# A two-block network on one core: loads, matmul order and PSUM banks of the first five projection slabs changed

## The reference, cut to what matters

```python
def rms_norm(x, g):
    xf = x.astype(jnp.float32)
    y = xf * lax.rsqrt(jnp.mean(xf * xf, axis=-1, keepdims=True) + NORM_EPS)
    return (y * g.astype(jnp.float32)).astype(x.dtype)

def hybrid_layer(x, ...):
    hn = rms_norm(x, ln1)
    proj = hn @ w_in          # 1024 -> 2824 columns: queries, keys, values, mLSTM inputs and gates
    mq, mk, mv, sq, sk, sv, xqk, xv, xo, xi, xf = jnp.split(proj, idx, axis=-1)
    ...
    x = x + jnp.concatenate([y_moba, y_mlstm, y_swa], axis=-1) @ w_out
    u = rms_norm(x, ln2) @ w_up
    return x + jnp.square(jax.nn.relu(u)) @ w_down
```

## Time and profile before

| | us |
|---|---|
| median of three runs (1414.11 to 1416.08) | 1415.93 |
| the profiled execution | 1415.56 |
| its span, from the first instruction to the last | 1413.8 |
| TensorE busy | 1389.7 (98%) |
| VectorE busy | 1119.7 (79%) |
| ScalarE busy | 845.9 (60%) |
| GpSimd busy | 101.3 (7%) |

### The profile page before, as it was taken

One profiled execution on the slowest core, in us unless ns is written; L12 is line 12 of the kernel. 1 busy time (PEld: TensorE's weight loads), 2 busy tenths in 40 slices (PEclk: granted clock), 3 DMA queues, 4 the chain that ended last, 5 costly groups with the idle time before them and its releaser, 6 DMA issues.

```text
span 1413.8 us, 25601 instructions
## 1 busy us (share of the span) xinstructions
PE 1389.7 (98%) x10325; PEld 1301.2 (92%) x10325; DVE 1119.7 (79%) x1693; ACT 845.9 (60%) x1309; POOL 101.3 (7%) x157
## 2 busy tenths in 40 slices
PE   8999999999999999999999999999999999999997
PEld 7898888889888888889999999998999999999986
DVE  7898888889898888887777788777778777876653
ACT  6776776345876875356576475454465664754442
POOL 2000111100000011103100000000031000000000
PEclk9999999999999999999999999999999999999999
DMA  9643999986545999969955678887699456777662
GB/s 261 163 142 105 279 271 279 293 230 166 147 133 165 294 265 290 299 195 260 305 149 150 184 220 238 241 250 214 187 262 301 140 161 181 222 218 231 183 187 65
DMA packets 472692, 301.32 MB, mean 213 GB/s; under 512 B 15084, under 2 KB 453872, under 8 KB 472448
## 3 DMA queue, kind: packets, MB, share of 16 engines
q1 hardware_dynamic: 455056, 239.57, 60.7%
q0 software_dynamic: 16704, 58.29, 12.6%
q10 hardware_dynamic: 816, 1.84, 0.4%
HBM read 289.43 MB, written 1.05 MB: 205 GB/s over the span
## 4 chain that ended last, share of the span: by engine, by line
PE 85%; DVE 9%; ACT 4%; issue 2%; DMA 1%; SPq 0%; ACTq 0%; DVEq 0%
PE acc L2093 15%; PE acc L2094 15%; PE acc L2095 15%; PE mx L2110 10%; PE acc L2110 8%; PE mx L2111 5%; PE acc L2111 4%; DVE w_lo L1176 3%; DVE ada_acc L1266 1%; ACT w_hi L587 1%; PE acc L2125 1%; PE acc L2126 1%; PE acc L2127 1%; PE mx L2539 1%; PE acc L2231 1%
## 5 line engine op out<-in xcount | busy, mean ns | idle before, releaser
L1176 DVE TENSOR_TENSOR w_lo<-raw,w_hi 128x1024 fp32r<-128x1024 f32 x450 | 542.6, 1220 | 125.2 <-ACT w_hi L587 122.8
L587 ACT ACTIVATE w_hi<-raw 128x1024 fp32r<-128x1024 f32 x450 | 465.1, 1052 | 135.9 <-DMA raw<-in_w_in 63.4
L2093 PE MATMUL acc<-h,w_hi 128*128 128x256 f32 (+1 forms) x1696 | 484.5, 286 | 7.7 <-DVE w_lo L1176 5.5
L2094 PE MATMUL acc<-h,w_hi 128*128 128x256 f32 (+1 forms) x1696 | 475.6, 280 | 0.0
L2095 PE MATMUL acc<-h,w_lo 128*128 128x256 f32 (+1 forms) x1696 | 474.0, 280 | 0.0
L2093 PEld LDWEIGHTS acc<-h,w_hi 128*128 128x128 f32 x1696 | 319.4, 188 | 14.6 <-issue 7.8
L2094 PEld LDWEIGHTS acc<-h,w_hi 128*128 128x128 f32 x1696 | 319.7, 189 | 2.6 <-issue 2.4
L2095 PEld LDWEIGHTS acc<-h,w_lo 128*128 128x128 f32 x1696 | 320.2, 189 | 0.0
L2110 PE MATMUL mx<-u,w_hi 128*128 128x512 f32 x864 | 302.2, 392 | 0.0
L2111 PE MATMUL mx<-u,w_lo 128*128 128x256 f32 x864 | 243.5, 282 | 0.0
L2110 PEld LDWEIGHTS mx<-u,w_hi 128*128 128x128 f32 x864 | 162.2, 188 | 33.4
(11 more groups left out here) (309 smaller groups left out, 1667.9 us busy)
## 6 DMA issues: line engine op xcount, KB each, us to landing
raw<-in_w_in SPq DMA_DIRECT2D x132, 512.0 KB, 4.0
ada<-in_w_ada POOLq DMA_DIRECT2D x96, 512.0 KB, 5.6
raw<-in_w_ffn_in SPq DMA_DIRECT2D x88, 512.0 KB, 4.3
raw<-in_w_up SPq DMA_DIRECT2D x64, 512.0 KB, 5.2
raw<-in_w_down SPq DMA_DIRECT2D x64, 512.0 KB, 5.6
raw<-in_w_out SPq DMA_DIRECT2D x32, 512.0 KB, 3.8
raw<-in_w_ffn_out SPq DMA_DIRECT2D x32, 512.0 KB, 4.1
raw<-in_w_ret_o SPq DMA_DIRECT2D x16, 512.0 KB, 3.9
```

The costliest lines, as they stand in the source:

```text
L587: nc.scalar.activation(w_hi[:, n % NS], raw[:, n % NS], ACT.Copy).then_inc(hi_ready, 1)
L1176: V.tensor_tensor(w_lo[:, n % NS], raw[:, n % NS], w_hi[:, n % NS].bitcast(F32), ALU.subtract).then_inc(lo_ready, 1)
L2093: mm(outp, w_hi[:, i % NS, k], rhs[:, k, 0], start=k == 0, stop=False)
L2094: mm(outp, w_hi[:, i % NS, k], rhs[:, k, 1], start=False, stop=False)
```

## The change

SP issues the load of slab 0 between the two halves of x. On TensorE the transposes of x's second half come after eight products of slab 0 (its high part with high and low parts of tiles 0 to 3); slabs 0 and 1 are multiplied part by part (all high x high, high x low, low x high) and no longer tile by tile. `norm_sum` moves to the middle of slab 2. The gain vector is turned first, and four `keep_going` stand after the first half's transposes. VectorE copies the turned pairs 0, 1 and 2, ScalarE the last. ScalarE makes the high parts of slabs 4 and 5 after Ln and Exp; VectorE makes the low part of slab 2 between the sums of squares and that of slab 3 ahead of `norm_var`. In the first layer slabs 3 and 4 go to banks 3 and 2 of `mx`, which are idle then, and slabs 3 and 4 wait for no eviction. The diff, cut to its core:

```diff
+        first_bank = lambda l, i: mx[:, 6 - i] if l == 0 and i in (3, 4) else acc[:, i % 3]
...
                 sp.dma_start(xtok[:, :, half], x[0, :, half].rearrange("(t p) d -> p t d", p=P)).then_inc(s_x[n], 16)
+                if n == 0:
+                    load_columns(0, win_v, 0, A_ORDER[0] * P)
...
-            act.wait_ge(boot_t, 2)
-            nc.scalar.activation(xT[:, 2:4].rearrange("p k t -> p (k t)"), mx[:, 1], ACT.Copy).then_inc(x_second, 1)
-            act.wait_ge(x_second, 1)
             act.wait_ge(vec_ready, 1)
...
                     for k in range(KT):
-                        act.wait_ge(x_ready, (2, 2, 4, 6)[k // 2])
+                        if k == 4:
+                            act.wait_ge(boot_t, 5)
+                            nc.scalar.activation(xT[:, 6:8].rearrange("p k t -> p (k t)"), mx[:, 3], ACT.Copy).then_inc(x_last, 1)
+                        if k < 6:
+                            act.wait_ge(x_ready, (2, 4, 8)[k // 2])
+                        else:
+                            act.wait_ge(x_last, 1)
                         nc.scalar.activation(hd_hi[:, k], xT[:, k], ACT.Copy, scale=ln1_of(0)(k)).then_inc(n_hi, 1)
                         if k == 3:
                             ahead(0)
-                    act.wait_ge(x_ready, 8)
                     ahead(1)
                     for b in range(4):
+                        if b == 2:
+                            ahead(2)
                         if b == 3:
-                            ahead(2)
                             act.wait_ge(n_acc, 1)
...
-                ahead(5 if l == 0 else 7)
+                ahead(3 if l == 0 else 7)
                 norm_seed(l * 2)
...
-            tokens_turned(0)
-            dve.wait_ge(boot_t, 3)
+            dve.wait_ge(boot_t, 1)
             V.tensor_scalar(vecT[:, 0:V_LN2], acc[:, 3, 256:256 + V_LN2], float(D) ** 0.5, None, ALU.mult).then_inc(vec_ready, 1)
             dve.wait_ge(vec_ready, 1)
+            tokens_turned(0)
+            tokens_turned(1)
+            for k in range(4):
+                low_tile(0, k, ln1_of(0))
             tokens_turned(2)
-            tokens_turned(3)
-            low_tile(0, 0, ln1_of(0))
-            low_tile(0, 1, ln1_of(0))
             lo_upto(0)
-            dve.wait_ge(x_second, 1)
-            for k in range(2, KT):
-                low_tile(0, k, ln1_of(0))
+            low_tile(0, 4, ln1_of(0))
+            low_tile(0, 5, ln1_of(0))
+            dve.wait_ge(x_last, 1)
+            low_tile(0, 6, ln1_of(0))
+            low_tile(0, 7, ln1_of(0))
             lo_upto(1)
-            for b in range(4):
-                norm_squares(0, b)
+            norm_squares(0, 0)
+            norm_squares(0, 1)
+            lo_upto(2)
+            norm_squares(0, 2)
+            norm_squares(0, 3)
...
                 if l == 0:
+                    lo_upto(p0 + 3)
                     norm_var(0)
-                    lo_upto(p0 + 3)
                     norm_root(0)
...
+            def high_high(i, tiles):
+                pe.wait_ge(hi_ready, i + 1)
+                for k in tiles:
+                    if i == 0:
+                        pe.wait_ge(n_hi, k + 1)
+                    mm(acc[:, i, 0:S], w_hi[:, i, k], hd2[:, k, 0], start=k == 0, stop=False)
...
                 if b == 1:
...
+                    keep_going(4)
+                    high_high(0, range(4))
+                    high_low(0, range(4))
-            keep_going(4)
+            high_high(0, range(4, KT))
+            low_high(0, range(4))
+            high_low(0, range(4, KT))
+            low_high(0, range(4, KT)).then_inc(slab_used, 1)
+            high_high(1, range(KT))
+            high_low(1, range(KT))
+            low_high(1, range(KT)).then_inc(slab_used, 1)
...
-                        if i >= 3:
+                        if i >= (3 if l else 5):
                             pe.wait_ge(ap_ev, e0 + i - 2)
-                        slab(p0 + i, hd2, acc[:, i % 3, 0:S],
-                             before=(lambda k: pe.wait_ge(h_ready, l * 16 + k + 1)) if i == 0 else
-                             (lambda k: norm_sum(l * 2) if k == (4 if l else 7) else None) if i == 1 else None).then_inc(slab_used, 1)
+                        slab(p0 + i, hd2, first_bank(l, i)[:, 0:S],
+                             before=(lambda k: pe.wait_ge(h_ready, l * 16 + k + 1)) if l and i == 0 else
+                             (lambda k: norm_sum(l * 2) if k == 4 else None) if i == 2 - l else None).then_inc(slab_used, 1)
```

More of the change, by code:

```diff
@@ L458, in loads @@
                         elif j < A_PROJ:
-                            load_columns(i + j, win_v, l, A_ORDER[j] * P)
+                            if i + j:
+                                load_columns(i + j, win_v, l, A_ORDER[j] * P)
                         elif k < 0:
@@ L1313, in tokens_turned @@
             def tokens_turned(b):
-                dve.wait_ge(boot_t, b + 1 + (b >= 2))
-                V.tensor_copy(xT[:, 2 * b:2 * b + 2].rearrange("p k t -> p (k t)"), mx[:, b]).then_inc(x_ready, 2 if b < 3 else 4)
-                dve.wait_ge(x_ready, (2, 0, 4, 8)[b])
+                dve.wait_ge(boot_t, b + 2)
+                V.tensor_copy(xT[:, 2 * b:2 * b + 2].rearrange("p k t -> p (k t)"), mx[:, b]).then_inc(x_ready, 2 if b < 2 else 4)
+                dve.wait_ge(x_ready, (2, 4, 8)[b])
             def rest_of_vectors():
@@ L1352, in gates_to_sbuf @@
                     dve.wait_ge(slab_used, p0 + at + 1)
-                    c.done(V.tensor_tensor(gi[:], acc[0:4, at % 3, 0:S], rstd[0:4, 0:S], ALU.mult))
-                    V.tensor_tensor(gf[:], acc[32:36, at % 3, 0:S], rstd[32:36, 0:S], ALU.mult).then_inc(ap_ev, 1)
+                    c.done(V.tensor_tensor(gi[:], first_bank(l, at)[0:4, 0:S], rstd[0:4, 0:S], ALU.mult))
+                    V.tensor_tensor(gf[:], first_bank(l, at)[32:36, 0:S], rstd[32:36, 0:S], ALU.mult).then_inc(ap_ev, 1)
                     dve.wait_ge(ap_ev, e0 + at + 1)
@@ L1386, in to_sbuf @@
                         dve.wait_ge(slab_used, p0 + i + 1)
-                        V.tensor_tensor(proj[:, A_PLACE[A_ORDER[i]]], acc[:, i % 3, 0:S], rstd[:, 0:S], ALU.mult).then_inc(ap_ev, 1)
+                        V.tensor_tensor(proj[:, A_PLACE[A_ORDER[i]]], first_bank(l, i)[:, 0:S], rstd[:, 0:S], ALU.mult).then_inc(ap_ev, 1)
                 def convolve(j):
@@ L2153, in keep_going, with high_low, low_high @@
                     mm(acc[:, 2, S:], ident, con[:, 0:K_BLK], start=True, stop=True)
+            def high_high(i, tiles):
[4 more added lines that the diff above has]
+                    mm(acc[:, i, 0:S], w_hi[:, i, k], hd2[:, k, 0], start=k == 0, stop=False)
+            def high_low(i, tiles):
+                for k in tiles:
+                    if i == 0:
+                        pe.wait_ge(h_ready, k + 1)
+                    mm(acc[:, i, 0:S], w_hi[:, i, k], hd2[:, k, 1], start=False, stop=False)
+            def low_high(i, tiles):
+                pe.wait_ge(lo_ready, i + 1)
+                for k in tiles:
+                    ins = mm(acc[:, i, 0:S], w_lo[:, i, k], hd2[:, k, 0], start=False, stop=k == KT - 1)
+                return ins
             pe.wait_ge(s_con, 16)
             keep_going(3)
+            pe.wait_ge(s_ln1, 16)
+            nc.tensor.transpose(acc[:, 3, 256:256 + V_LN2], rows[0:V_LN2, 0], con[0:V_LN2, K_ID:K_ID + V_LN2]).then_inc(boot_t, 1)
             for b in range(4):
@@ L2166, in _ @@
                 if b == 1:
-                    pe.wait_ge(s_ln1, 16)
-                    nc.tensor.transpose(acc[:, 3, 256:256 + V_LN2], rows[0:V_LN2, 0], con[0:V_LN2, K_ID:K_ID + V_LN2]).then_inc(boot_t, 1)
-            keep_going(4)
+                    keep_going(4)
[8 more added lines that the diff above has]
+            low_high(1, range(KT)).then_inc(slab_used, 1)
             def rest_of_vectors():
@@ L2347, in up_slab @@
                     slab_both(m0 + k, h_part, acc[:, k % 4]).then_inc(slab_used, 1)
-                project(0, 1, 2)
+                if l:
+                    project(0, 1)
+                project(2)
                 if l == 0:
```

2 lines of the change are left out of this document (1 added, 1 removed).

## The result

The changed kernel takes 1419.67 us (median of five runs, 1419.22 to 1422.51) where the kernel before took 1415.54 on the same chip: ratio 1.0034, 95% interval 1.0021 to 1.0048. The forecast, 1416.6 and no change that can be told, was wrong, and its range (to 1418.9) too narrow. Run once more beside other kernels (e9) it was 1418.74 against 1414.98, 1.0026 [1.0016, 1.0037].

The account below looks back on a forecast made before the run. It took VectorE's list to gate_rows, then TensorE, as the bound. The root's +0.70 us, with the same 19.3 behind it, carried the median from 1415.93 to 1416.6, no change that can be told; range 1413.9 to 1418.9.

Parts of the forecast that it names:

- Transposes as before, the first copy at 6.86.: Start of the kernel: transposes of x's first half unchanged, the first copy at 6.86, taking 0.69 us.
- Transfers: Start: with the loads swapped slab 0 lands at 8.7 us (bounds 7.7 and 10.26), x's second half at 10.26.
- Rival 4: The swapped load lands no earlier than 10.26, slab 0's high part starts 1.1 us later: +1.8, 1417.7; chance 0.05.
- Eight products, then the second half: Start, TensorE: products 10.27 to 11.20, second transposes to 12.3, x's second half ready 3.5 us later, slab 1's high part 14.43.
- Slabs 0 to 2, the later sum: TensorE: slab 0's last product 0.96 us earlier, but 15 more matmuls ahead of the sum cost 1.75; sum at 21.41.
- VectorE to the marker: VectorE's steps up to the root of rstd (L1181): var at 21.44, root at 22.80, 0.70 us later.
- so I take full clock: TensorE, 8.9 to 13.4 us: its longest pause is shorter than the one that cost the clock, so no fall.
- rival 1: TensorE's clock falls once, a matmul taking 0.215 from 12.8 to 16.3: root 23.48, +1.38, 1417.3; chance 0.28.
- What it wins by 40 us it then stands waiting ... at gate_rows.: TensorE leaves slab 2 at 22.6; its lead is spent waiting for VectorE's evictions or at gate_rows, listed as costing nothing.
- The sum: Whole kernel: root +0.70, same 19.3 us behind it, gate_rows at 42.25, TensorE full to the end: median 1416.6.
- rival 2: TensorE's clock stays low through slab 1, 24 matmuls at 0.215 instead of 0.117: +3.7, 1419.6; chance 0.09.
- Rival 3: VectorE's list has hidden slack, so slab 2's end counts, 22.6 against 23.6: -1.0, 1414.9; chance 0.12.

Follow-up runs that it names:

- e9: The kernel after, without an edit, run once more beside other kernels: 1418.74 us against 1414.98, ratio 1.0026.
- e13: The kernel before, without an edit, run for a second profile: -0.15 us against before, ratio 0.9998.
- e11: The kernel after with filler matmuls in the start's pauses, ahead of gate_rows and before the first constants land: +3.28 us over before, ratio 1.0021.
- e10: The kernel after with filler matmuls in the start's pauses and ahead of gate_rows: +3.54 us over before, ratio 1.0025.
- e2: The kernel after with three filler matmuls ahead of gate_rows in the first layer: +3.13 us over before, ratio 1.0020.
- e4: The kernel after with the transposes of x's second half ahead of the eight products: +0.46 us over before, ratio 1.0004.
- the filled kernels: Kernels with fillers in TensorE's pauses, transposes first against products first: +1.34 against +3.28 and +0.63 against +3.54 us over before.
- e3: The kernel after with norm_sum right behind slab 1, no longer within slab 2: +2.10 us over before, ratio 1.0011.
- e14: The kernel before with the start filled, the root's first step done six times more and fillers in TensorE's pause: +4.26 us over before, ratio 1.0031.
- e8: The kernel after with slabs 3 and 4 back in the three banks of acc: +2.70 us over before, ratio 1.0018.

## Why the prediction was wrong, step by step

**The base.** "It ran at 1.00 through 6.09 to 10.49, idled 2.17", and the low stretch behind it, were taken as the kernel's; they were one execution's. The usual root is 21.27, not 22.10, so the change was charged 0.83 too little. Nothing in the one trace contradicted it, but its own row showed a fall in the very stretch that the change rewrites, and the kernel before was then worked out in one of its two cases only.

**"Transposes as before, the first copy at 6.86."** Failed: 7.43, as the transposes ran at the lower clock. Swapping the loads had taken away what hid this (slab 0, landing at 10.1 in e13). e11, with these transposes at full pace, has the root 0.34 earlier than e10, from which it differs in nothing else, and 0.42 earlier than e2.

**Transfers.** Right, and better than forecast: slab 0 lands 5.9 after its issue, at 7.6 (forecast 8.7, lower bound 7.7). Rival 4 falls. It bought less than it could, as the high part of slab 0 then waits for ScalarE's tiles (9.86).

**Eight products, then the second half.** The mechanism was right and was named as "the price of this order": slab 1's high part at 15.18, forecast 14.43, and all of it on the path. What was missed is that its price outweighed the swap's gain: e4 shows 1.94 at the root, the filled kernels 1.9 to 2.9 us of time.

**Slabs 0 to 2, the later sum.** The price was right for TensorE's path: the 12 matmuls that e3 takes out (48 instead of 60) are 1.4 at 0.117 apart. That the two paths meet was right too: in e2 VectorE's low part ends at 22.21 and the sum at 22.25. So at full clock the late sum costs nothing at the root; e3's 1.42 to 1.52, against e9 and the kernel after, is the fall's 1.55 hidden behind VectorE, and its likeness to 1.4 is chance.

**VectorE to the marker.** "From var to the root passes 1.36", bare: measured 1.36 in the kernel after, e2 and e4. "The same 19.3 behind it": 25.21 to 44.54, 19.3. Small steps came 0.44 late in sum (e11's root 23.24 against 22.80).

**Clock, "so I take full clock".** Failed in both profiles: low from 15.77, 1.55 at the root. The choice compared the longest single pause with the one before; here pauses of 0.62 and 1.17 were followed by a fall, while e2's of 1.23 and 1.17 were not: the length of a pause was no measure, as the waits of 1.69 without a fall show too. The Trainium skill (TensorE: Matmul & The Clock Gate, Part 4: PE-mode transpose) says that a transpose does not count as TensorE work as a matmul does, and rival 1 was its case. A fall did come, at 15.77, where rival 1 had it at 12.8. But e2, with the same transposes and products in the same order, has none, so the rule alone doesn't decide it here, and no run isolates what transposes count for.

**"What it wins by 40 us it then stands waiting ... at gate_rows."** Right, 1.13; but put under what costs nothing, with "then TensorE full to the end". That step failed: the wait was followed by the second low stretch, +1.55, in both profiles and, by the mean clocks, in most timed runs, and no rival held it.

**The sum.** Profile against profile, with e13 as the base, the root's +3.94 is 0.70 as forecast, 0.83 base, 0.44 small steps, 0.42 between e11 and e2 (0.34 of it the slow first transposes), 1.55 fall at the start. From there to the end: 1.55 second fall, 0.95 later waits, 6.4 in all (1412.8 to 1419.2). In the medians, by e2, it is the forecast's 0.70, 1.79 more at `gate_rows` (base, small steps, transposes), 0.64 behind it, and 0.6 to 1.0 for the falls that e2 takes out.

**Rivals.** The time is rival 2's (1419.6), its mechanism is not: from 19.18 the clock was full, and some six matmuls of slab 1 ran low, not 24. Rival 3 falls: no lead carried through. Rival 1 is part of it, with a fall of 1.55 where it had 0.71.

**What stays open.** The medians moved by 4.13 and 3.76, the profiles by 6.4: the profiled execution of the kernel after is 1.34 above its median, e13's 0.97 below. Taking the falls out (e2, e10, e11) left +3.1 to +3.5; 2.1 to 2.5 of that is the shift at `gate_rows` against e13, and the rest came later, as in e14, from a cause that was not followed to its end. In the timed runs the falls seem worth about 1 us, where each costs 1.55 in a profile. The mean clocks say which are common: in e2, e3 and e8, whose start is unfilled, 26 of 34 timed runs stand at 0.998 or above and so have no fall at the start, while 8 of 12 runs of the kernel after, with `gate_rows` unfilled too, have one. So the fall at the start, part of the profiles' sum, was rare in the runs that gave the medians. Why a fall comes in one execution and not in the next stays open.

## What to carry to other kernels

Where one profile shows the clock falling in the stretch that a change rewrites, work out the kernel before both with and without that fall. On an engine that runs in order, put the step that feeds other engines ahead of work that only feeds itself: eight products ahead of eight transposes cost more than the earlier load gave. Where an edit wins just what its count of matmuls promised, look which path it won it on: e3 won back a fall of the clock, and not the matmuls. A lead that must be spent waiting is not free, and a delay may arrive at the end longer than it set out.

## What the runs showed of the hardware

TensorE's full clock came at 6.02 in one profile of the kernel before and at 8.67 in another of the same code; transposes at the lower clock follow one another in 0.21 instead of 0.11 us. A wait of 1.1 us ahead of four matmuls of 4 rows was followed by a stretch at half clock in four of five profiles, while two pauses of 1.2 us at the start of e2, one of 1.33 in e8 and ones of 1.69 among full matmuls in every profile were followed by none. In two profiles of kernels that differ by a delay of 2.86 us at 41 us, the same 512 KB loads took 4.7 to 5.0 us and 7.6 to 7.8 us, and the spans are 4.0 apart.
